# Fourth chunk's mixer weights: loaded raw and split by GpSimd instead of read back as two stored tiles

## The reference, cut to what matters

```python
u = rms_norm(h, g_pre_mix[i]); z = u @ w_in[i]
z_glu, q, k, v, z_gate = jnp.split(z, split_at, axis=-1)
c = a * jax.nn.sigmoid(b)                       # a, b: halves of z_glu
c = causal_depthwise_conv(c, conv_dw_w[i], conv_dw_b[i])
y_conv = jax.nn.silu(layer_norm(c, conv_ln_g[i], conv_ln_b[i])) @ w_conv_out[i]
y_attn = sliding_window_sink_attention(q, k, v, attn_sinks[i]) @ w_attn_out[i]
y = gates[:, :, 0, :] * y_conv + gates[:, :, 1, :] * y_attn
h = h + rms_norm(y @ w_out[i], g_post_mix[i])
u = rms_norm(h, g_pre_ffn[i]); gate, val = jnp.split(u @ w_up[i], 2, axis=-1)
...
```

## Time and profile before

| | before |
|---|---|
| median of 3 runs | 2740.63 us (2739.75 to 2743.52) |
| the profiled execution | 2739.87 us, span 2738.1 us |
| TensorE (PE) busy | 2639.4 us, 96% of the span |
| VectorE (DVE) busy | 1629.3 us, 60% |
| GpSimd (POOL) busy | 1556.7 us, 57% |
| ScalarE (ACT) busy | 808.0 us, 30% |
| HBM read and written | 413.87 MB and 150.99 MB, 206 GB/s over the span |
| granted clock of TensorE, mean | 0.989 of full speed |

### The profile page before, as it was taken

One profiled execution on the slowest core, in us unless ns is written; L12 is line 12 of the kernel. 1 busy time (PEld: TensorE's weight loads), 2 busy tenths in 40 slices (PEclk: granted clock), 3 DMA queues, 4 the chain that ended last, 5 costly groups with the idle time before them and its releaser, 6 DMA issues.

```text
span 2738.1 us, 32299 instructions
## 1 busy us (share of the span) xinstructions
PE 2639.4 (96%) x11772; PEld 2156.4 (79%) x11772; DVE 1629.3 (60%) x2211; ACT 808.0 (30%) x1405; POOL 1556.7 (57%) x1876
## 2 busy tenths in 40 slices
PE   9999899988998999999999999999799999999989
PEld 6888677767787878888888878877588888888877
DVE  8975679565976797766545501268844555401286
ACT  2542342333424452433322220022322222310031
POOL 6678233333332000389888843388788888733487
PEclk9999999999999999999999999999899999999999
DMA  7778877888787746544444564355244444743535
GB/s 283 271 259 317 307 253 258 284 276 282 255 273 281 259 161 226 192 159 172 169 169 162 193 244 158 130 178 181 98 154 161 148 160 152 266 184 121 192 118 176
DMA packets 270782, 567.02 MB, mean 207 GB/s; under 512 B 22560, under 2 KB 112928, under 8 KB 270496
## 3 DMA queue, kind: packets, MB, share of 16 engines
q1 hardware_dynamic: 239952, 485.25, 51.9%
q10 hardware_dynamic: 30672, 79.71, 7.6%
HBM read 413.87 MB, written 150.99 MB: 206 GB/s over the span
## 4 chain that ended last, share of the span: by engine, by line
PE 65%; DMA 14%; DVE 8%; POOL 8%; issue 2%; SPq 1%; ACT 1%; DVEq 0%; ACTq 0%
DMA up_quad<-in_up_raw 12%; PE ps L1440 10%; PE ps L1442 10%; PE ps L1446 10%; PE ps L1223 9%; PE ps L1219 8%; PE ps L1220 8%; DVE ps L1778 2%; POOL up_quad L693 2%; POOL up_quad L691 2%; POOL up_quad L695 2%; POOL up_quad L689 2%; PE ps L1209 2%; PE ps L1211 2%; PE ps L1210 2%
## 5 line engine op out<-in xcount | busy, mean ns | idle before, releaser
L679 POOL TENSOR_TENSOR w_lo<-w_stage,w_hi 128x256 fp32r<-128x256 f32 (+1 forms) x1200 | 1023.7, 883 | 25.6
L675 POOL CAST w_hi<-w_stage 128x1024 fp32r<-128x1024 f32 (+2 forms) x320 | 354.2, 1107 | 747.1 <-DMA w_stage<-up_sums 363.3
L1440 PE MATMUL ps<-comb_hi,w_hi 128*128 128x512 f32 x1232 | 481.6, 391 | 18.2 <-ACT ple_sg L1051 13.1
L1442 PE MATMUL ps<-comb_lo,w_hi 128*128 128x512 f32 x1232 | 481.2, 391 | 0.0
L1446 PE MATMUL ps<-comb_hi,w_lo 128*128 128x512 f32 x1232 | 329.9, 390 | 2.1 <-POOL w_lo L679 2.1
L1778 DVE SCALAR_TENSOR_TENSOR ps<-conv_in,col,ps 128x512 f32<-128x512 f32 x436 | 294.4, 746 | 0.8
L1440 PEld LDWEIGHTS ps<-comb_hi,w_hi 128*128 128x128 f32 x1232 | 232.2, 188 | 68.2 <-ACT ple_sg L1051 13.5
L1219 PE MATMUL ps<-ring_hi,w_hi 128*128 128x512 f32 x704 | 274.3, 390 | 5.5 <-DMA ring_lo<-f_kept 5.5
L1220 PE MATMUL ps<-ring_lo,w_hi 128*128 128x512 f32 x704 | 274.1, 389 | 0.0
L1446 PEld LDWEIGHTS ps<-comb_hi,w_lo 128*128 128x128 f32 x1232 | 231.9, 188 | 50.8 <-POOL w_lo L679 2.5
L1442 PEld LDWEIGHTS ps<-comb_lo,w_hi 128*128 128x128 f32 x1232 | 232.2, 189 | 48.2
(11 more groups left out here) (251 smaller groups left out, 4647.5 us busy)
## 6 DMA issues: line engine op xcount, KB each, us to landing
w_hi<-split_weights SPq DMA_DIRECT2D x138, 512.0 KB, 4.3
w_lo<-split_weights SPq DMA_DIRECT2D x138, 512.0 KB, 5.1
w_stage<-up_sums SPq DMA_DIRECT2D x176, 256.0 KB, 2.9
w_stage<-in_weights SPq DMA_DIRECT2D x86, 512.0 KB, 4.6
w_stage<-in_up_raw SPq DMA_DIRECT2D x132, 256.0 KB, 2.9
split_weights<-w_hi SPq DMA_DIRECT2D x46, 512.0 KB, 2.8
split_weights<-w_lo SPq DMA_DIRECT2D x46, 512.0 KB, 4.0
up_quad<-in_up_raw SPq DMA_DIRECT2D x88, 256.0 KB, 3.3
```

The lines of the kernel that those rows point to most:

```text
L675: nc.gpsimd.tensor_copy(w_hi[:, slot, 0:many], w_stage[:, slot, 0:many]).then_inc(w_hi_ready, 1)
L679: last = nc.gpsimd.tensor_tensor(w_lo[:, slot, k:end], w_stage[:, slot, k:end], w_hi[:, slot, k:end].bitcast(F32), ALU.subtract)
L1440: nc.tensor.matmul(ps[:, bank], w_hi[:, slot, first + k], comb_hi[i][:, k], start=start and k == 0, stop=False, skip_group_check=True)
L1442: nc.tensor.matmul(ps[:, bank], w_hi[:, slot, first + k], comb_lo[i][:, k], start=False, stop=False, skip_group_check=True)
```

## The change

`SPLIT` becomes true for the fourth chunk's mixer blocks as well. Nothing else is edited: what depends on `SPLIT` follows it, which is the load (one DMA of 512 KB in place of two), the 46 splits in GpSimd's queue, the counts of the semaphores, and TensorE's order in `full_block`, `by_tile` and `attention_outs`. `KEPT` stays as it was, so nothing more is stored.

```diff
 for _n, (_c, _b) in enumerate(ORDER):
-    _split = _b >= B_WP or _c == 0
+    _split = _b >= B_WP or _c in (0, CHUNKS - 1)
     _kept = _b < B_WP and _c == 0
     _count += _split
```

## The result

The kernel before took 2740.2 us in the median beside the changed one (2738.0 to 2743.5), the changed one 2775.7 us (2770.4 to 2780.7): a ratio of 1.0128, with an interval of 1.0107 to 1.015. The change makes the kernel slower by about 1.3%. In a second comparison, with its own runs of the kernel before, the ratio was 1.0100 (1.0076 to 1.0123). The forecast was 2762.0 us, within 2743 to 2776; so the sign and the mechanism were right, and the size was too small.

What follows compares the result with a forecast made beforehand. TensorE was taken as the bound, VectorE as the engine with small margins. Terms 3.0 + 4.5 + 3.0 + 7.0 + 4.4 - 0.5 = 21.4 us on the median gave 2762.0 us; own range 2748 to 2774, with rivals 2743 to 2776.

Steps and rivals of the forecast that it cites:

- rival 3: Fourth mixer: GpSimd becomes the bound as well, 8 to 12 us on top, 2770 to 2774 us; chance 0.10.
- rival 1: Fourth chunk: splits stay hidden, VectorE's margins of 2.4, 2.3 and 9.9 us hold, 2740 to 2745 us; chance 0.12.
- (d): Combined inputs at the mixer's end: VectorE's contended steps make `first_a` late; 7.0 us, bounds 1 and 11.
- rival 2: Faster by the saved traffic, with waits gone and VectorE unhurt: at most 5.2 us, 2735.5 us; chance 0.03.
- (a): POST sum at the fourth chunk's start: slower angle steps and `s_lo` hold up TensorE; 3.0 us, bounds 0.5 and 4.7.
- (b): PRE sum: 17 two-input VectorE steps grow beyond a 2.4 us margin; 4.5 us, bounds 0 and 6.3.
- (c): Attention and taps: slower normalisations, tiny steps and taps on SBUF accumulators; 3 us, bounds 0.5 and 4.5.
- (e): Half clock for 4 to 6 us behind TensorE's longer stops: two falls of three, 4.4 us, bounds 0 and 9.

Runs made afterwards that it cites:

- e_pool_read: Kernel before, stored tiles and loads kept, plus GpSimd work with a split's reads and writes in the fourth mixer, result unused: ratio 1.0091.
- e_head: Kernel before with the change only in the fourth mixer's first 14 blocks (GLU, q, k, v): ratio 1.0034.
- e_mid: Kernel before with the change only in the fourth mixer's 24 blocks of the gates and the attention: ratio 1.0027.
- e_pool_write: Kernel before plus four GpSimd memsets, which read nothing, for each of the fourth mixer's 46 blocks: ratio 1.0013.
- e_tail: Kernel before with the change only in the fourth mixer's 8 blocks of w_out: ratio 1.0030.
- e_spread: Kernel before with the up weights' 88 sum steps spread over 132 blocks, a third moved to the fourth chunk: 2706.3 us, ratio 0.9864.

## Why the prediction was right, and where its sizes were off

The steps that held: VectorE is the engine to look at; two-input steps go from 0.61 to 1.23 us beside a split, taps stay at 747 ns; GpSimd keeps up (no wait on `w_hi` or `w_lo` in the mixer, so rival 3 is out), VectorE's margins of 2 us don't hold (rival 1 out), and the saved traffic takes nothing off TensorE's time but what is said at (d) (rival 2 out: e_pool_read loses nearly the same with all of it). One slip without effect: 46 blocks of 512 KB are 24.1 MB, as measured, and not 23.6. Term by term, from the profile of after:

- **(a) POST sum**, forecast 3.0: the wait went from 1.42 to 6.79 us, 5.4. The share of contended time was too small: all nine steps and `s_lo` were hit, not two thirds. The nine steps and `s_lo` took 10.7 us instead of 5.7, 5.0 more, above the upper bound of 4.7.
- **(b) PRE sum**, forecast 4.5: TensorE's waits there are 0.6 us (2.8 in the second profile and in e_head). Two steps failed. The share of contended time was too large: the forecast's 17 steps and the add of L1675 took 12.4 us before and 17.0 in after, 4.6 of the 11.2 that 0.62 us each would make, a share of 0.41 (0.64 in the other two) instead of 0.8. And it was added to the clock's loss, while the two run side by side: from the end of one `s_lo` to the start of the next VectorE took 30.6 us instead of 24.8, 3.4 us more than the margin of 2.4, and TensorE, at a clock of 0.91 from 893 to 924 us, needed 2.9 us more for its own products. Together A to B grew by 8.9 us (11.2 in the second profile and in e_head), beside 3.0 + 4.5 + 2.2 = 9.7 forecast: the sum came near by luck, a term too small and one too large.
- **(c) Attention and taps**, forecast 3.0 (0.5 to 4.5): B to C grew by 7.9 us (10.5 in the second profile, 6.2 in e_mid alone). This is the term that was mis-sized. I took the growth of a normalisation from chunk 0, 0.19 us; in after it is 1034 - 692 = 342 ns (135 ns in e_mid). That isn't a larger share of GpSimd's time: it is busy 33.4 of 57 us in chunk 0's attention and 36.2 of 62 us here. A mean over eight steps depends on which of them meet an instruction of GpSimd's: five did in chunk 0, six do here, and the longest took 1.09 and 1.45 us. And the "tiny ones" weren't tiny in time: `s_den`'s additions of 128x4 went from 154 to 385 ns. In e_pool_write, beside memsets, and in e_head, where GpSimd splits nothing at that place, all eight stay at 143 to 166 ns. The trace of before already had this price in chunk 0, 90 to 155 us:

```profile
L1858 DVE TENSOR_TENSOR s_den<-s_den,s_sinke 128x4 f32<-128x4 f32 x8 | 2.8, 346 | 1.7 <-ACT s_sinke L787 1.7
```

Four taps that start on an SBUF accumulator went from 754 to 1038 ns. 8 x 0.34 + 8 x 0.23 + 4 x 0.28 = 5.7 us, and TensorE's waits from B to C grew by the same 5.7 us, from 0.6 to 6.3. About 1.7 us more come from a fall of the clock that the forecast didn't have here: 0.89 from 1045 to 1060 us, behind the 2.8 us on the taps. DVE's groups in after, 916 to 1050 us:

```profile
L1860 DVE TENSOR_TENSOR prob<-prob,s_rec 128x512 f32<-128x512 f32 x8 | 8.3, 1034 | 0.3
...
L1778 DVE SCALAR_TENSOR_TENSOR ps<-conv_in,col,conv_acc 128x512 f32<-128x512 f32 x4 | 4.0, 1038 | 1.1 <-ACT v_even L779 1.1
...
L1858 DVE TENSOR_TENSOR s_den<-s_den,s_sinke 128x4 f32<-128x4 f32 x8 | 3.1, 385 | 1.8 <-ACT s_sinke L787 1.7
```

- **(d) Combined inputs and (e) the clock behind them**, forecast 7.0 + 2.2 - 0.5 = 8.7: C to D grew by 10.5 us (9.7 in e_tail). The forecast's working held. The 35 steps that it listed took 42.7 us instead of 22.1, 20.6 of the 21.7 at full contention (it took 19.5). `s_lo`'s 1.6 us vanished, and TensorE's stop of 9.56 us with half the clock behind it came. The wait for the stored tiles fell from 5.50 to 1.98 us, half of it since the four differences ahead were 1.8 us longer; counted from the memset ahead of them (L1686), the tiles' differences begin 1.7 us earlier, the one thing that the saved traffic gave. In e_pool_read, with all traffic, they begin 8.1 us behind that memset, as before (8.3), and C to D is 2.1 us longer than in after. Whether it would shrink with `first_a` ahead of the last combined inputs in ScalarE's queue wasn't tried.
- **The clock** fell behind (a) and (d), two of the three stops that (e) names, and once more in (c). In 890 to 915 us it is 0.83, in 1160 to 1200 us 0.87, and 1.00 in both stretches before. The forecast took 4.33 us as the size of stop that such a fall follows, from the earlier trace rows. In the runs it followed shorter ones too: 2.8 us in (c), and 1.9 us in e_spread; behind the stop of 1.42 us of before it stayed at 1.00.

Forecast 21.4; A to D 27.3 us. The 5.9 us between them are (c)'s 4.9 and (d)'s 1.8 less 0.8 of the head. The median, 2775.7 us, lies 0.3 us inside the range, and that owes something to luck. The forecast's own range ended at 2774; the last 2 us were taken in for rival 3, which the runs rule out. On the other side, 8 us of the difference of the two profiles are the scatter ahead of A and behind D, and in the second comparison the loss was 27 us. The upper bound of (c), 4.5 us, was too low in every profile of the change (6.2 to 10.5 us).

## What to carry to other kernels

Giving an idle engine work wasn't free here, since its reads slowed the engine that has the small margins: list that engine's instructions by where their inputs lie, and price each two-input step at up to one whole instruction of the newcomer, however small the step is. Lateness of an engine that runs without a pause is one backlog over all the waits behind it; reordering one step moves the wait. Before traffic is saved, look where a product waits for a load: there thinning out a side stream by a third gave 1.4%, while saving 24 MB elsewhere cost 1.3%. And a term that a trace can price is better read than guessed: the small additions stood in the trace of before at 346 ns.

## What the runs showed of the hardware that I had not expected

- A VectorE addition of 128x4 takes 154 ns alone and 385 ns in the mean beside splits, with single ones at 684 ns (1001 ns in e_mid). The 0.53 us that such a one adds is near the 0.62 us that a remainder of 128x512 loses, so the loss doesn't shrink with the step's own size.
- A remainder took 11.65 / 8 = 1.46 us beside copies, 0.85 more than alone, where a copy takes 1.16 us in the mean over the mixer; beside splits it lost 0.62 us, where a subtraction alone takes 2.82 / 4 = 0.70 us. So it is less than a whole undisturbed instruction each time. GpSimd is slowed as well: its copies beside these remainders took 10.07 / 7 = 1.44 us, so the two engines go nearly step for step, one remainder to one copy.
- GpSimd's memsets, which read nothing, can more than double VectorE's fast one-input steps (0.49 to 1.14 us) and leave the two-input ones at 0.69.
